# Turning five blocks of constants at another place in the mixer of a four-block decoder

## The chip, the cores and the metric

The kernel runs on one core of one Trainium2 chip. The metric is the time on the device, in microseconds (us), of one execution; the lower, the better.

## What is computed

Two stacks of two layers each run over 256 tokens of width 1024, in float32. Only the first mixer matters here. With `h = rmsnorm(x)` and `p = h @ ev_w_in`, the first 1024 columns of `p` feed a gated block (`u`, `va`), the others a linear recurrence (RWKV-7) over 8 heads of 64:

```python
def rwkv7_time_mix(p, mu, w0, w2, a0, a2, g2, k_k, k_a, r_k, gn_g, gn_b):
    p = p + (shift_prev(p) - p) * mu
    r, k, v, lw, la, lg = split(p)
    w = -softplus(-(w0 + tanh(lw) @ w2)) - 0.5
    decay = exp(-exp(w)); a = sigmoid(a0 + la @ a2); g = sigmoid(lg) @ g2
    kk = heads(k * k_k); kk = kk * rsqrt(max(sum(kk * kk, -1), 1e-24))
    k = k * (1.0 + (a - 1.0) * k_a)
    ...                       # the recurrence over time, then a group norm
    bonus = sum(rh * kh * r_k, -1) * vh
    return (o + bonus) * g
```

The layers behind it use small constant vectors: the weights and biases of a causal convolution (`ff_conv_w`, `ff_conv_b`, `conv_w_2`) and the bias `b_ada_2` of a modulation.

## The kernel before, in words

Each engine has a hand-written queue and works it off in order; semaphores tie them together. The sync engine's queue loads the weights, two megabytes at a time, into two ring buffers. Each chunk is used in halves. ScalarE copies a half in a rounded format (`split_hi`, line 601), VectorE computes the remainder (`split_lo`, line 607), and TensorE multiplies with both parts, three matmuls of 256 columns for one exact product, 48 for a whole half (`pe_tile`, lines 1032 to 1034; `pe_rows`, lines 1047 to 1049). Each call of `w.go()` makes the half that is three ahead of the one about to be used: the halves are, by number, 0 for `lora`, 1 and 2 for `k`, 3 and 4 for `va`, 5 and 6 for `r`, 7 and 8 for `u`, 9 and 10 for `v`, 11 to 14 for the output projection.

The small constants are loaded as rows at the start, in seven blocks (`PRS`, line 647). The kernel needs them down the partitions, so TensorE turns each block (`pe_column`, line 772) into a PSUM bank and VectorE copies it from there into `COL` (`dve_column`, line 778). Blocks 6 and 0 are turned at the very start. Blocks 1 to 5 (three of the convolution's weights, its biases, `b_ada_2`) are first used behind the mixer.

The order of TensorE's queue in the mixer is: `lora`, `k` (2 halves), the small matmuls of the two low-rank gates (`sg`, line 2167), the first half of `va`, the sums of the keys' squares (`nm`, line 2175, which wait for ScalarE's squares of line 1301), the gate `g` (line 2182), the second half of `va`, `r` (2), `ws` (line 2191), `u` with the spatial mix `ya` between (lines 2199, 2204), the first half of `v`, blocks 1 to 5, the bonus sums `rk` (line 2214, two matmuls), the second half of `v`, and the turned `v` (`vt`, line 2222). Then comes the solve of the recurrence, TensorE's small matmuls of lines 2235 to 2396.

PSUM banks are given out ahead of time by `bank_plan`. A ring of six banks (0 to 5) serves the keys in the order in which the plan lists them, and `opened(e, key)` makes TensorE wait until the key that had the bank before has been read out. So the place of a key in the list decides who waits for whom. In the kernel before, in the plan's order:

```
key    rk0  rk1   v1    vt0   vt1
bank   0    1     2     3     4
before v0   col1  col2  col3  col4      (the key that had the bank before)
```

`v0` is read out by VectorE's `mixed(5)` (line 1692), which follows ScalarE's `mixed(5)` (line 1272) in the first half of `v`. The columns are read out by `dve_column`, which stands in VectorE's queue behind the `split_lo` that follows `mixed(5)`, and that one waits for ScalarE's `split_hi` behind its own `mixed(5)`.

GpSimd waits for all seven blocks (`col_turned`) before it writes unit matrices over the place where the rows lay (`tt_eye`, line 1222), then for the bonus sums (`rk_mm`), then for the last half of `v`.

Of the kernel before, what the change touches and what calls it, by code (L numbers as in the profile page):

```python
# [104 lines left out]
TWO = [(n, q) for n in range(2) for q in range(2)]  # L105
# [193 lines left out]
def bank_plan():  # L299
# [12 lines left out]
    norm(0, r, False)  # L312
    P.use(("va", 0), 6)
    P.use(("va", 1), 7)
    for key in [("col", 0), ("lora", 0), ("k", 0), ("k", 1), *(("sg", w, q) for q, w in TWO), ("nm", 0), ("nm", 1),
                ("g", 0), ("g", 1), ("r", 0), ("r", 1), "ws", ("u", 0), ("ya", 0), ("ya", 1), ("u", 1), ("v", 0),
                *(("col", t) for t in range(1, 6)), ("rk", 0), ("rk", 1), ("v", 1), ("vt", 0), ("vt", 1)]:
        P.use(key, r())
    r = Ring(range(8))
    for n in range(2):  # L320
# [121 lines left out]
def program(nc, A, consts, out):  # L442
    with ExitStack() as ctx:
# [61 lines left out]
        def ht(k):  # L505
            return HT1 if k else HT0
# [10 lines left out]

        S = Sems(lambda name: ctx.enter_context(nc.semaphore(name)))
        bank_of = bank_plan()
        bank_sems = [S[f"bank{b}"] for b in range(8)]  # L520

# [4 lines left out]
        def ps_of(key):  # L526
            return PS[bank_of[key][0]]

        def bank_sem(key):
            return bank_sems[bank_of[key][0]]  # L530

        def opened(e, key):
            b, n = bank_of[key]
            if n:
                e.wait_ge(bank_sems[b], n)
            return PS[b]
# [4 lines left out]
        for n, (key, parts) in enumerate(chunks):  # L541
# [5 lines left out]
            if len(parts) == 2:  # L547
                v = r[:, :].rearrange("p (s k n) -> p s k n", s=2, k=NK)
# [20 lines left out]
        def shaped(x, k):  # L569
            if k == NK:  # L570
                return c3(x, NK)
            if k:
                return x.rearrange("p (s k n) -> p s k n", s=2, k=NK)
            return x
# [28 lines left out]
        def split_lo(e, which):  # L603
            for i in which:
                n, v, k, _ = halves[i]
                e.wait_ge(S["w_hi"], i + 1)
                e.tensor_tensor(shaped(WLO[i % NB], k), v, shaped(WHI[i % NB], k).bitcast(F32),  # L607
                                ALU.subtract).then_inc(S["w_lo"], 1)
# [8 lines left out]
        def taken(e, w):  # L617

            i = w.taken
            w.taken += 1  # L620
            e.wait_ge(S["w_lo"], i + 1)
            return WHI[i % NB], WLO[i % NB]
# [10 lines left out]
        col, row_parts, n_rows = {}, [], []  # L633
# [134 lines left out]
        def pe_column(e, t):  # L768
            ps = opened(e, ("col", t))
            e.wait_ge(S[f"rows{t}"], 16 * len(row_parts[t]))  # L770
            k = n_rows[t]
            e.transpose(ps[:, 0:k], PRS[t][0:k, :], CT[0:k, C_ID:C_ID + k]).then_inc(S["col_turned"], 1)
# [3 lines left out]
        def dve_column(e, t):  # L776
            e.wait_ge(S["col_turned"], COL_ORDER.index(t) + 1)
            e.tensor_copy(COL[:, t * 128:t * 128 + n_rows[t]],
                          ps_of(("col", t))[:, 0:n_rows[t]]).then_inc(bank_sem(("col", t)), 1)
# [237 lines left out]
        def flat_k(w, k):  # L1017
            return w[:, 256 * k:256 * k + 256]

        def pe_tile(e, w, key, k_norm, fresh, pair=False, turned=()):  # L1020

            hi, lo = taken(e, w)
            ps = opened(e, key)
            h = ht(k_norm)
            for a in range(2):
                o = ps[:, 256 * a:256 * a + 256]
                for k in range(NK):
                    if fresh and a == 0 and k % 4 == 0:
                        e.wait_ge(S["h_lo"], 4 * k_norm + 3 + k // 4)
                    c = (8 * a + k) * 128 if pair else 256 * k + 128 * a  # L1030
                    wh, wl = hi[:, c:c + 128], lo[:, c:c + 128]
                    e.matmul(o, wh, h[0][:, k, :], start=k == 0, stop=False)  # L1032
                    e.matmul(o, wh, h[1][:, k, :], start=False, stop=False)  # L1033
                    x = e.matmul(o, wl, h[0][:, k, :], start=False, stop=k == NK - 1)  # L1034
                if a == 0 and turned:
                    pe_turn_back(e, k_norm, turned)
            x.then_inc(S["w_used"], 1)

        def pe_rows(e, w, key, k_norm, q):

            hi, lo = taken(e, w)
            h = ht(k_norm)
            for n in range(2):
                ps = opened(e, key(n)) if q == 0 else ps_of(key(n))
                o, t = ps[:, 256 * q:256 * q + 256], slice(128 * n, 128 * n + 128)
                for k in range(NK):
                    e.matmul(o, h[0][:, k, t], flat_k(hi, k), start=k == 0, stop=False)  # L1047
                    e.matmul(o, h[0][:, k, t], flat_k(lo, k), start=False, stop=False)  # L1048
                    x = e.matmul(o, h[1][:, k, t], flat_k(hi, k), start=False, stop=k == NK - 1)  # L1049
            x.then_inc(S["w_used"], 1)  # L1050
# [621 lines left out]
        def vector_program(e):  # L1672
            w = Stream()
# [11 lines left out]
            def mixed(m):  # L1685

                name, o, mu0, q = MIXED[m]
                ps = ps_of((name, q))
                e.wait_ge(S["mix_own"], m + 1)
                for a in range(2):  # L1690
                    t = o[:, 2 * q + a, 1:256]
                    x = e.scalar_tensor_tensor(t, ps[:, 256 * a:256 * a + 255], cc("ev_mu", mu0 + 2 * q + a), t,
                                               ALU.mult, ALU.add)
                x.then_inc(bank_sem((name, q)), 1)
# [23 lines left out]
            e.tensor_tensor(E1, SS[:, :, 0, 64], SS[:, :, 0, 128], ALU.subtract).then_inc(S["e1"], 1)  # L1718
            e.wait_ge(S["e1"], 1)
            e.tensor_tensor(E2, E1, SS[:, :, 1, 64], ALU.subtract).then_inc(S["e2"], 1)  # L1720
            split_lo(e, w.go())
            for q in range(2):
                key = ("nm", q)
# [15 lines left out]
            for n in range(2):  # L1739
                s6, q = st6[:, 6 * n:6 * n + 6], mv[:, 4 * n:4 * n + 4]  # L1740
# [6 lines left out]
            for n in range(2):  # L1747
                q, key = mv[:, 4 * n:4 * n + 4], ("va", n)
# [26 lines left out]
            for q in range(2):  # L1775
                key = ("u", q)
# [14 lines left out]
                                ALU.subtract).then_inc(S["ya_lo"], 1)  # L1791
            mixed(5)
            split_lo(e, w.go())
            for t in range(1, 6):
                dve_column(e, t)
            mixed(6)
            for q in range(2):
                key, v = ("rk", q), Vm[:, 2 * q:2 * q + 2, :]
# [5 lines left out]
            for n in range(2):  # L1804
                for g in range(2):
                    key = ("L", n, g)
# [24 lines left out]
            for i in range(1, 6):  # L1831
                for n in range(2):
                    key = ("Y", i, n)
# [96 lines left out]
            for what, p in OD:  # L1930
                two, t = slice(2 * p, 2 * p + 2), pairs[p % 4]
# [3 lines left out]
                elif what == "s":  # L1935
# [4 lines left out]
                    for g in range(2):  # L1940
                        key = ("od", "s", 2 * p + g)
# [28 lines left out]
            for what, i in MO:  # L1970
# [4 lines left out]
                elif what == "kn":  # L1975
                    k = KR[:, i]
# [6 lines left out]
                    for n in range(2):  # L1983
                        key = ("kr", n) if i else ("first", 4, n)
                        e.tensor_tensor(c3(XN[:, n, 512 * i:512 * i + 512], 4), c3(ps_of(key)[:, :], 4),
                                        bc(k[:, n, :], 128), ALU.mult).then_inc(bank_sem(key), 1)
                elif what == "rq":
                    key = ("rq", i)
# [6 lines left out]
                elif what == "p":  # L1995
                    t = smx[i % 4]
# [6 lines left out]
                elif what == "lo":  # L2003
                    key = ("mo", "o", i)
# [8 lines left out]
            for hh in range(2):  # L2013
                for p in CIN_PART:
                    for q in range(2):
                        key, j = ("cin", p, hh, q), 2 * q
# [6 lines left out]
                        if p == 2:  # L2023
# [3 lines left out]
                            for a in range(2):  # L2027
                                k = m = 4 * hh + j + a
                                u, t = CG[:, j + a, :], CV[:, j + a, :]
# [6 lines left out]
                        elif p == 0:  # L2036
                            k, v = 4 * hh + j, CV[:, j:j + 2, :]
# [112 lines left out]
        def tensor_program(e):  # L2150
            w = Stream()
# [9 lines left out]
            for q in range(2):  # L2161
# [6 lines left out]
                                     LOR[p, 0, :], start=True, stop=True)  # L2168
                x.then_inc(S["lora_mm"], 1)
            pe_rows(e, w, lambda n: ("va", n), 0, 0)  # L2170
            e.wait_ge(S["consts_in"], 16)
            for q in range(2):
                ps = opened(e, ("nm", q))
# [32 lines left out]
                x.then_inc(S["ya_mm"], 1)  # L2206
            pe_tile(e, w, ("u", 1), 0, False)
            pe_tile(e, w, ("v", 0), 0, False)
            for t in range(1, 6):
                pe_column(e, t)  # L2210
            for q in range(2):
                ps = opened(e, ("rk", q))
                e.wait_ge(S["rk_in"], 1)
# [90 lines left out]
            for n in range(2):  # L2304
                key = ("Y64", n)
# [11 lines left out]
            for n in range(2):  # L2317
                key = ("TT64", n)
# [112 lines left out]
            for what, p in OD:  # L2431
# [22 lines left out]
                elif what == "o":  # L2454
# [4 lines left out]
                    for n, c, start, stop in ((0, 0, True, True), (0, 1, True, False), (1, 2, False, True)):  # L2459
                        t = slice(128 * min(c, 1), 128 * min(c, 1) + 128)  # L2460
                        for g in range(2):
                            v = slice(128 * p + 64 * g, 128 * p + 64 * g + 64)
# [111 lines left out]
        @block.vector  # L2574
        def _(e):
            vector_program(e)

        @block.tensor
        def _(e):
            tensor_program(e)  # L2580
# [28 lines left out]
```

## Time and profile before

| | us |
|---|---|
| median of 3 runs (lowest, highest) | 1316.14 (1311.34, 1316.25) |
| the profiled execution | 1313.9 |
| its span, from the first to the last instruction | 1312.1 |
| TensorE busy (share of the span) | 1258.2 (96%) |
| VectorE busy | 944.9 (72%) |
| ScalarE busy | 711.8 (54%) |
| GpSimd busy | 16.8 (1%) |

Busy time is the time in which an engine has at least one instruction in work. Matmuls are pipelined, so their busy times overlap, and what a matmul costs in a row of them is the distance from its start to the next start. PE is TensorE, PEld its weight load, DVE VectorE, ACT ScalarE, POOL GpSimd, SP the sync engine. A float32 matmul that is not split by hand stands in the records as two.

### The profile page before, as it was taken

Reading aid. Unit: us, or ns where it says so; the run is one execution under the profiler, and the core shown is the slowest. Engines: PE = TensorE matmul, PEld = TensorE weight load, DVE = VectorE, ACT = ScalarE, POOL = GpSimd, SP = SyncE. Lnnn points to the kernel's source line nnn. Section 1 sums busy time; section 2 is a strip of 40 time slices with the busy share of each in tenths; the row PEclk is TensorE's granted clock in tenths of the full one; section 3 lists DMA queues with packets and bytes.
Section 4 is the critical chain, followed back from the end, with each engine's and each line's share of the span. In section 5 each row is a group of like instructions: output and inputs, shape, how many; then the busy total and the mean of one; then the engine's idle time right before and its main releaser. Section 6 shows DMA issues by size and latency. Waiting matters only on the chain.

```text
span 1312.1 us, 24165 instructions
## 1 busy us (share of the span) xinstructions
PE 1258.2 (96%) x10251; PEld 1171.3 (89%) x10251; DVE 944.9 (72%) x1268; ACT 711.8 (54%) x1039; POOL 16.8 (1%) x26
## 2 busy tenths in 40 slices
PE   6988999999999999999999998999999999999998
PEld 5877879999989888999998997899998898899997
DVE  5784347988877776988877566699997676677543
ACT  5932447665555566865556555644444654744442
POOL 0002000000000000000000000000000000000000
PEclk9999899999999999999999999999999999999999
DMA  9450227777557526677653535599995365675550
GB/s 315 153 193 2 67 62 260 251 237 237 205 194 258 192 65 206 225 266 239 221 211 104 185 129 181 205 326 340 358 343 210 126 233 188 213 263 182 181 184 32
DMA packets 161572, 263.77 MB, mean 201 GB/s; under 512 B 3565, under 2 KB 95929, under 8 KB 161466
## 3 DMA queue, kind: packets, MB, share of 16 engines
q1 hardware_dynamic: 160586, 259.54, 57.7%
q10 hardware_dynamic: 880, 2.69, 0.7%
q8 instruction: 81, 1.33, 0.4%
q14 instruction: 25, 0.20, 0.0%
HBM read 261.17 MB, written 1.05 MB: 200 GB/s over the span
## 4 chain that ended last, share of the span: by engine, by line
PE 73%; DVE 12%; ACT 5%; DMA 5%; issue 4%; DVEq 0%; SPq 0%; ACTq 0%
PE ps L1061 19%; PE ps L1032 12%; PE ps L1034 12%; PE ps L1033 12%; DVE wlo L607 4%; DVE acc L2079 4%; PE ps L2257 2%; DMA arena<-in_w_ada_dram 2%; ACT whi L601 2%; PE ps L1047 1%; PE ps L1049 1%; PE ps L1048 1%; PE ps L818 1%; PE ps L820 1%; PE ps L819 1%
## 5 line engine op out<-in xcount | busy, mean ns | idle before, releaser
L607 DVE TENSOR_TENSOR wlo<-ring,whi 128x2048 fp32r<-128x2048 f32 x195 | 445.5, 2288 | 114.3 <-ACT whi L601 113.2
L1032 PE MATMUL ps<-ghi,whi 128*128 128x256 f32 x1600 | 449.1, 281 | 0.6 <-DVE wlo L607 0.6
L1034 PE MATMUL ps<-ghi,wlo 128*128 128x256 f32 x1600 | 446.8, 279 | 0.0
L1033 PE MATMUL ps<-glo,whi 128*128 128x256 f32 x1600 | 446.8, 279 | 0.0
L601 ACT ACTIVATE whi<-ring 128x2048 fp32r<-128x2048 f32 x195 | 372.3, 1914 | 96.4 <-PE ps L1061 61.6
L1032 PEld LDWEIGHTS ps<-ghi,whi 128*128 128x128 f32 x1600 | 300.2, 188 | 1.5 <-DVE wlo L607 0.8
L1033 PEld LDWEIGHTS ps<-glo,whi 128*128 128x128 f32 x1600 | 300.0, 188 | 0.7
L1034 PEld LDWEIGHTS ps<-ghi,wlo 128*128 128x128 f32 x1600 | 300.3, 188 | 0.0
L1061 PE MATMUL ps<-whi,yhi 128*128 128x512 f32 x480 | 159.4, 397 | 4.2 <-DVE ylo L1916 1.3
L1061 PE MATMUL ps<-wlo,yhi 128*128 128x512 f32 x480 | 156.3, 391 | 0.0
L1061 PE MATMUL ps<-whi,ylo 128*128 128x512 f32 x480 | 155.9, 390 | 0.0
L2079 DVE SCALAR_TENSOR_TENSOR acc<-arena,small,acc 128x512 f32<-128x512 f32 x168 | 126.2, 751 | 7.1 <-DMA arena<-in_w_ada_dram 1.9
L1061 PEld LDWEIGHTS ps<-whi,yhi 128*128 128x128 f32 x480 | 88.3, 188 | 23.9 <-issue 4.2
L1061 PEld LDWEIGHTS ps<-whi,ylo 128*128 128x128 f32 x480 | 90.2, 188 | 19.3
L1061 PEld LDWEIGHTS ps<-wlo,yhi 128*128 128x128 f32 x480 | 90.4, 188 | 19.0
L2121 DVE SCALAR_TENSOR_TENSOR arena<-arena,cols 128x254 f32<-128x254 f32 (+1 forms) x176 | 74.5, 480 | 20.8 <-ACT arena L1642 19.8
L818 PE MATMUL ps<-whi,ghi 128*128 128x256 f32 x224 | 63.9, 285 | 7.0 <-DVE glo L960 6.9
L2136 DVE TENSOR_TENSOR ylo<-arena,yhi 128x256 fp32r<-128x256 f32 x88 | 37.1, 422 | 44.9 <-ACT yhi L1659 44.7
L1640 ACT ACTIVATE arena<-ps 128x512 f32<-128x512 f32 x44 | 26.3, 598 | 73.5 <-PE ps L1034 71.8
L1646 ACT ACTIVATE arena<-ps 128x256 f32<-128x256 f32 x44 | 16.8, 381 | 84.9 <-PE ps L1034 84.8
L819 PE MATMUL ps<-wlo,ghi 128*128 128x256 f32 x224 | 62.7, 280 | 0.0
L820 PE MATMUL ps<-whi,glo 128*128 128x256 f32 x224 | 62.7, 280 | 0.0
(311 smaller groups left out, 1625.0 us busy)
## 6 DMA issues: line engine op xcount, KB each, us to landing
arena<-in_w_ada_dram SPq DMA_DIRECT2D x48, 1024.0 KB, 6.4
ring<-in_ff_w_up_dram SPq DMA_DIRECT2D x44, 1024.0 KB, 7.6
ring<-in_w_gate_up_dram SPq DMA_DIRECT2D x44, 1024.0 KB, 7.1
ring<-in_ff_w_down_dram SPq DMA_DIRECT2D x10, 2048.0 KB, 7.9
ring<-in_w_down_dram SPq DMA_DIRECT2D x10, 2048.0 KB, 8.1
ring<-in_od_w_qkv_dram SPq DMA_DIRECT2D x6, 2048.0 KB, 7.8
ring<-in_w_qkv_dram SPq DMA_DIRECT2D x6, 2048.0 KB, 7.9
ring<-in_w_in_dram SPq DMA_DIRECT2D x6, 2048.0 KB, 8.0
```

The costliest lines, as they stand in the source:

```text
L601: e.activation(shaped(WHI[i % NB], k), v, ACT.Copy).then_inc(S["w_hi"], 1)
L607: e.tensor_tensor(shaped(WLO[i % NB], k), v, shaped(WHI[i % NB], k).bitcast(F32), ALU.subtract).then_inc(S["w_lo"], 1)
L818: e.matmul(o, h[0][:, c, t], wh, start=c == 0, stop=False)
L819: e.matmul(o, h[0][:, c, t], wl, start=False, stop=False)
L820: x = e.matmul(o, h[1][:, c, t], wh, start=False, stop=c == NK - 1)
L1032: e.matmul(o, wh, h[0][:, k, :], start=k == 0, stop=False)
L1033: e.matmul(o, wh, h[1][:, k, :], start=False, stop=False)
L1034: x = e.matmul(o, wl, h[0][:, k, :], start=False, stop=k == NK - 1)
L1061: x = e.matmul(ps[:, :], YT[l][:, src_k + i, t], w[r][:, i, 512 * h:512 * h + 512], start=first, stop=last)
L2079: e.scalar_tensor_tensor(a, AW[:, k, :], SC[:, k:k + 1], a, ALU.mult, ALU.add).then_inc(S["ada_acc"], 1)
L2121: e.scalar_tensor_tensor(t[a][:, lag:256], z[:, 256 * a:256 * a + 256 - lag], conv_col(f, 2 - lag, a * NF + p), t[a][:, lag:256], ALU.mult ...
L2136: e.tensor_tensor(YT[1][:, p % 8, :], tg[r], YT[0][:, p % 8, :].bitcast(F32), ALU.subtract).then_inc(S["y_lo"], 1)
```

## The change

Blocks 1 to 5 are turned by TensorE, and copied by VectorE, at another place of their queues, and stand at another place of the bank plan: behind the low-rank gates and ahead of the sums of the keys' squares. In TensorE's queue that is behind the first half of `va`, in VectorE's behind the small sums `E1`, `E2` (lines 1718, 1720) and ahead of the `split_lo` of half 6. Nothing else is edited.

```diff
@@ bank_plan
-    for key in [("col", 0), ("lora", 0), ("k", 0), ("k", 1), *(("sg", w, q) for q, w in TWO), ("nm", 0), ("nm", 1),
+    for key in [("col", 0), ("lora", 0), ("k", 0), ("k", 1), *(("sg", w, q) for q, w in TWO), *(("col", t) for t in range(1, 6)), ("nm", 0), ("nm", 1),
                 ("g", 0), ("g", 1), ("r", 0), ("r", 1), "ws", ("u", 0), ("ya", 0), ("ya", 1), ("u", 1), ("v", 0),
-                *(("col", t) for t in range(1, 6)), ("rk", 0), ("rk", 1), ("v", 1), ("vt", 0), ("vt", 1)]:
+                ("rk", 0), ("rk", 1), ("v", 1), ("vt", 0), ("vt", 1)]:
@@ vector_program
             e.tensor_tensor(E2, E1, SS[:, :, 1, 64], ALU.subtract).then_inc(S["e2"], 1)
+            for t in range(1, 6):
+                dve_column(e, t)
             split_lo(e, w.go())
@@ vector_program
             mixed(5)
             split_lo(e, w.go())
-            for t in range(1, 6):
-                dve_column(e, t)
             mixed(6)
@@ tensor_program
             pe_rows(e, w, lambda n: ("va", n), 0, 0)
+            for t in range(1, 6):
+                pe_column(e, t)
             e.wait_ge(S["consts_in"], 16)
@@ tensor_program
             pe_tile(e, w, ("u", 1), 0, False)
             pe_tile(e, w, ("v", 0), 0, False)
-            for t in range(1, 6):
-                pe_column(e, t)
             for q in range(2):
                 ps = opened(e, ("rk", q))
```

The bank plan that follows from it, in the plan's order, from the moved blocks on:

```
key    col1 col2 col3  col4  col5  nm0   nm1  g0   g1   r0   r1   ws   u0   ya0  ya1
bank   1    2    3     4     5     0     1    2    3    4    5    0    1    2    3
before k0   k1   sg0,0 sg1,0 sg0,1 sg1,1 col1 col2 col3 col4 col5 nm0  nm1  g0   g1

key    u1   v0   rk0   rk1   v1    vt0   vt1
bank   4    5    0     1     2     3     4
before r0   r1   ws    u0    ya0   ya1   u1
```

From `rk0` on every key has the bank that it had in the kernel before.

## Rows read from the trace of the kernel before

**Rows 1.** The page's first part: busy time, share of the span, instructions.

```profile
PE 1258.2 (96%) x10251; PEld 1171.3 (89%) x10251; DVE 944.9 (72%) x1268; ACT 711.8 (54%) x1039; POOL 16.8 (1%) x26
```

**Rows 2.** Chain that ended last, 86 to 110 us: start, us, what.

```profile
88.38 0.47 ACT mix L1272
88.85 1.81 ACT whi L601
90.68 2.29 DVE wlo L607
92.97 0.17 DVE cols L778
```

**Rows 3.** Timeline, 87 to 102 us: start, us, engine, line, out<-in, idle before.

```profile
87.69 0.28 PE L1034 MATMUL ps<-hhi,wlo 128*128 128x256 f32 x1
...
87.81 0.57 PE L772 MATMUL ps<-consts_sb,pre 88*128 88x88 f32 x5
...
88.97 0.87 DVE L1692 SCALAR_TENSOR_TENSOR mix<-ps,cols,mix 128x255 f32<-128x255 f32 x2
...
89.89 1.12 PE L2214 MATMUL ps<-pre,consts_sb 128*128 128x512 f32 x2 [1.50 <-DVE mix L1692]
...
93.19 1.82 PE L2214 MATMUL ps<-pre,consts_sb 128*128 128x512 f32 x2 [2.17 <-DVE cols L778]
...
101.28 0.28 PE L1034 MATMUL ps<-hhi,wlo 128*128 128x256 f32 x1
```

**Rows 4.** Windows: length, busy of PE, PEld, DVE, ACT, POOL, granted clock, DMA.

```profile
44.20:45.65 1.45, 0.00 (x1) 0.03 (x1) 1.45 (x5) 1.44 (x4) 0.00 (x0) 1.00 1.02 390
...
88.40:93.20 4.80, 1.14 (x3) 0.31 (x3) 3.95 (x7) 2.25 (x3) 1.63 (x2) 1.00 0.89 290
93.50:96.90 3.40, 3.40 (x12) 2.44 (x11) 0.29 (x2) 0.00 (x0) 1.18 (x2) 0.50 0.56 176
...
103.70:107.10 3.40, 3.24 (x16) 2.95 (x15) 0.05 (x1) 0.72 (x2) 1.55 (x2) 0.50 0.00 0
```

**Rows 5.** Timeline, 41 to 49 us, around the keys' squares.

```profile
41.67 1.62 ACT L1294 ACTIVATE mix<-ps,cols 128x256 f32<-128x256 f32 x4
...
43.88 0.28 PE L1049 MATMUL ps<-whi,hlo 128*128 128x256 f32 x1
44.60 1.71 ACT L1301 ACTIVATE pre<-mix,cols 128x256 f32<-128x256 f32 x4
...
45.65 1.96 PE L2175 MATMUL ps<-pre,consts_sb 128*128 128x512 f32 x4 [1.49 <-ACT pre L1301]
...
46.21 0.17 DVE L1720 TENSOR_TENSOR small<-small,pre 128x4 f32<-128x4 f32 x1
...
47.44 1.89 PE L2182 MATMUL ps<-pre 128*128 128x256 f32 x8
...
48.13 2.29 DVE L607 TENSOR_TENSOR wlo<-ring,whi 128x2048 fp32r<-128x2048 f32 x1 [1.76 <-ACT whi L601]
```

**Rows 6.** Timeline of the sync engine's queue: issue of the last block's rows.

```profile
10.48 0.35 SPq L647 DMA_DIRECT2D pre<-in_b_ada_dram  x1
```

**Rows 7.** The area that holds the rows, by tile: its transfers, from issue to landing.

```profile
DMA to landing us min/median/max: 7.0/7.8/8.4
```

**Rows 8.** Timeline of VectorE, 92 to 94 us: the five copies.

```profile
92.89 0.90 DVE L778 COPY cols<-ps 128x88 f32<-128x88 f32 x5
```

**Rows 9.** Timeline of VectorE, 77 to 82 us.

```profile
77.38 1.67 DVE L1772 SCALAR_TENSOR_TENSOR pre<-mix,cols 128x256 f32<-128x256 f32 x4
...
81.35 0.68 DVE L1780 TENSOR_TENSOR xn<-xn,ps 128x512 f32<-128x512 f32 x1
```

**Rows 10.** Timeline of TensorE, first and last of the 48 matmuls of half 7.

```profile
66.48 0.36 PE L1032 MATMUL ps<-hhi,whi 128*128 128x256 f32 x1
...
72.11 0.28 PE L1034 MATMUL ps<-hhi,wlo 128*128 128x256 f32 x1
```

**Rows 11.** Timeline of TensorE, 103 us: the turned v.

```profile
103.44 3.50 PE L2222 MATMUL ps<-consts_sb,mix 128*128 128x128 f32 x16 [1.88 <-issue]
```

## The prediction

> **What bounds the kernel now.** I read the page's first part first: TensorE is busy for 96% of the span, VectorE for 72%, ScalarE for 54% [rows 1]. So only idle time or slow time of TensorE can give anything back, and the question is whether the five moved blocks cause such time. Next I asked for the chain of waits around the place they are taken from. Between the end of the first half of v and the second sum of the bonus it leaves TensorE: ScalarE's own share of v (0.47 us), ScalarE's rounding of half 13 (1.81), VectorE's remainder of half 13 (2.29), and the first column copy (0.17) [rows 2]. None of this is data that the bonus sums need. The timeline shows how it gets onto the path [rows 3]. The last matmul of half 9 starts at 87.69, the five transposes follow at 87.81, then TensorE waits twice: 1.50 us for bank 0, which v0 holds until mixed(5) is done, and 2.17 us for bank 1, which column block 1 holds. The last matmul of half 10 starts at 101.28.
>
> The windows add a third loss [rows 4]. In the 4.8 us from 88.4 to 93.2 TensorE worked for 1.14 us, and from 93.5 to 96.9, when it was busy throughout, its granted clock was 0.50, the 1.2 GHz level; in the gap at 44.2 to 45.65 it stayed at 1.00, the 2.4 GHz level.
>
> **What is added at the new place.** TensorE's last matmul of va's first half starts at 43.88; the keys' sums start at 45.65, after 1.49 us of idle time that ScalarE's squares end [rows 5]. Five transposes took 0.57 us [rows 3], in front of which their banks must be free and their rows there. Rows: the last block is issued at 10.48 [rows 6], the slowest landing of that area took 8.4 us [rows 7], so by 18.9, 25 us early. Banks: blocks 1 and 2 follow k0 and k1, blocks 3 to 5 follow gates; the last gate's read ends at 41.67 + 1.62 = 43.29 [rows 5], and that is a gate whose bank only nm0 takes. So the transposes run from 44.2 to 44.8 and cost nothing; the cover is the wait for the squares, 0.9 us of it is left, and without it they would cost 0.57.
>
> VectorE finishes its small sums at 46.21 + 0.17 = 46.38 and then idles 1.76 us for ScalarE's half 6, until 48.13 [rows 5]. Five column copies took 0.90 us [rows 8]: 46.3 to 47.2, hidden, 0.9 us to spare; without cover, 0.90 on VectorE.
>
> The one new wait on TensorE is nm1's, for bank 1, which block 1 now holds until its copy is done. Four records of the two sums span 45.65 to 47.44, so 0.90 us each, and nm1 began at about 46.55. The copy of block 1 begins at 46.3 to 46.4 and takes a quarter of a microsecond (five overlapping ones make 0.90), so it ends near 46.6 and TensorE follows at 46.65. Cost: 0.1 us. Bounds: 0 if the copy slips in behind line 1720 at once; 0.3 if it starts only at 46.6. Behind nm1 stand g0 (bank 2, block 2, copied by 46.8, wanted at 47.5), g1 (bank 3, block 3, copied by 47.0, wanted at 48.4) and r0, r1 (blocks 4, 5, wanted much later): no cost. Behind these copies on VectorE stands only half 6. SP's queue is passed by nothing and issues nothing more. On GpSimd the unit matrices that wait for all seven columns are written right behind the gates instead of behind 88 us; it is busy for 1% of the span and waits for the bonus sums next, so nothing moves there.
>
> **What is removed at the old place.** After half 9 the bonus sums come at once. Their input (line 1772) is ready at 77.38 + 1.67 = 79.05. rk0 gets bank 0 from ws, read long before; rk1 gets bank 1 from u0, read at 81.35 + 0.68 = 82.03 [rows 9]. Half 10 gets bank 2 from ya0, whose read has to be over before line 1780 can run. Its weights are no condition: the remainder made at 90.68 is three halves ahead, half 13. Step by step:
>
> - rk0 starts where the first transpose stood, 87.81, plus the 0.1 us from nm1: 87.91.
> - The two sums take 47.44 - 45.65 = 1.79 us at the full clock [rows 5]: half 10 starts at 89.70.
> - From the first to the last of 48 matmuls it is 72.11 - 66.48 = 5.63 us at the full clock [rows 10]: the last starts at 95.33.
> - Before, it started at 101.28 [rows 3]. The gain is 5.95 us.
>
> As a cross-check by terms: idle 1.50 + 2.17, the transposes' own part 0.58 (88.39 less 87.81), and half the 3.4 us at half clock, 1.70, make 5.95, and 0.1 goes off for nm1: 5.85. The two agree within 0.1; I take 6.0 as a round number, bounds 5.6 (nm1 at 0.3, a slower start of half 10) and 6.3.
>
> Is it kept? Half 10 is followed by mixed(6) on ScalarE and VectorE. ScalarE is free from 88.85 + 1.81 = 90.66, VectorE from 92.97 once the column copies behind it are gone [rows 2]; they are wanted from 95.6. So VectorE's margin is about 3 us. The solve behind it is one chain from TensorE to the copies and back, fed by no transfer, so it moves forward whole; the later weight loads are released by halves used up, and move with it.
>
> **How this stands to the times.** The span of 1312.1 us has 1.8 us around it, 1313.9 in all: 1313.9 - 6.0 = 1307.9. The median of the runs shown, 1316.14, lies 2.2 above the profiled execution, and less 6.0 it gives 1310.1. I have no reason to favour either and take the middle, 1309.0.
>
> **Rivals.**
>
> *The clock also stays up for the turned v.* The 16 records of line 2222 took 3.50 us [rows 11], at a granted clock of 0.50 [rows 4]. They are 8 matmuls of 128 columns, as many columns as the two sums that took 1.79 us at full clock, so the low level cost 1.7 us here. It came after an idle stretch of 1.88 us; one of 1.49 us at 44.2 brought no fall. In the changed kernel the same 1.88 us follow 7.5 us of work (87.8 to 95.3) without a gap, and if the clock holds, the gain is 7.7 us: 1313.9 - 7.7 = 1306.2. Against it: the idle stretch itself is not shorter, and the last 4.6 us before it were fully busy before too. The Trainium skill ("TensorE: Matmul & The Clock Gate", The HAM clock gate) says that the activity monitor runs freely and doesn't start with the kernel, so that one kernel pays a different number of slow matmuls from run to run. By that rule this 1.7 us comes and goes in both kernels, and only a part of it would show between medians; the trace of one execution can't show it.
>
> *Half 10 must wait for its weights.* If the remainder made at 90.68 were half 10's own and not three ahead, it would start at 92.97, not 89.70: 3.3 us less, a gain of 2.7, 1311.2 from the profiled time. For it speaks only that this remainder stands right in front in the chain [rows 2]; against it, the count of halves.
>
> *The gain is given back later in the mixer.* VectorE or GpSimd, not TensorE, would have to end the next wait. VectorE's margin of 3 us speaks against it. It would leave anything from 0 to 3 us; at 0 the time is 1313.9 to 1316.1.
>
> *Slower: a column's rows are late.* TensorE's queue is in order, so a row block that has not landed by 45.65 holds the keys' sums and all behind them, one for one. It eats the whole gain from 45.65 + 6.0 = 51.65 on and makes the kernel slower by over 0.5% from about 58 on, 39 us later than the landing worked out above. I see nothing that could do it.
>
> **Chances and range.** The forecast (gain 5 to 7) gets 0.55, the clock as well (7 to 8.5) 0.25, weights 0.05, given back 0.12, slower 0.03. The low end is the clock case from the profiled time, 1306.2, less 1.2 because medians of this kernel have runs 5 us apart: 1305.0. The high end is the weight case from the median, 1316.14 - 2.7 = 1313.4. What a measurement can tell from no change is about 0.5%, 6.6 us. That lies inside the forecast's own range: against the median of 1316.14 the predicted 1309.0 is 7.1 us less (0.54%), while the gain as summed is 6.0 (0.46%). So I give the forecast half to each side: faster 0.25 + 0.27 = 0.52, same 0.28 + 0.05 + 0.12 = 0.45, slower 0.03.
>
> **What would show it.** Right: five transposes between 44.2 and 44.8 with the keys' sums still at 45.65; column copies at 46.3; no idle time of TensorE between half 9 and half 10 and a clock of 1.00 there; rk1's wait gone from the chain; the last matmul of half 10 near 95.3. Wrong: an idle row in front of nm1 of more than 0.3 us; half 10 released by VectorE's remainder at 93.0; mixed(6) starting late behind 95.6 although its matmul is done; or later stages that start less than 6 us earlier, with an idle row that was not there before. A line 2222 of 1.8 us would be the clock's case.

## The result, and the profile after

The changed kernel took 1305.11 us (median of 8 executions, 1302.08 to 1308.58) against 1312.49 for the kernel before (8 executions, the three shown earlier among them, 1310.0 to 1316.6). The ratio is 0.9934, with a 95% interval of 0.9918 to 0.9951: 0.66% faster, which is 8.7 us of 1312; the medians lie 7.4 us apart. It went the way that was forecast and by the steps that were named, but by more than the 6.0 us that were summed, and from a lower level: 1309.0 plus 6.0 puts the kernel before at 1315.0, and 86 executions of it, taken together, average 1313.5. One execution in all that follows, 1342.79 us with the fillers at the bonus sums, lies 2.5% above the others of its kernel and counts in no ratio or mean, only in that kernel's median.

The page's first line of the changed kernel has TensorE 4.4 us less busy at the same count of instructions [rows 1]:

```profile
PE 1253.8 (96%) x10251; PEld 1167.9 (90%) x10251; DVE 944.3 (72%) x1268; ACT 711.6 (55%) x1039; POOL 15.9 (1%) x26
```

Timeline of the changed kernel around the keys' squares, for [rows 5] (L2177 is the keys' sums, L2184 the gate g):

```profile
43.48 0.28 PE L1049 MATMUL ps<-whi,hlo 128*128 128x256 f32 x1
...
43.59 0.58 PE L772 MATMUL ps<-consts_sb,pre 88*128 88x88 f32 x5
...
45.44 2.07 PE L2177 MATMUL ps<-pre,consts_sb 128*128 128x512 f32 x4 [1.26 <-ACT pre L1301]
...
46.08 0.90 DVE L778 COPY cols<-ps 128x88 f32<-128x88 f32 x5
...
47.34 1.89 PE L2184 MATMUL ps<-pre 128*128 128x256 f32 x8
...
47.92 2.29 DVE L607 TENSOR_TENSOR wlo<-ring,whi 128x2048 fp32r<-128x2048 f32 x1 [0.94 <-ACT whi L601]
```

The transposes stand in the wait, which is still ended by ScalarE's squares. They began 0.6 us sooner than the 44.2 of the prediction: 0.4 because TensorE was that much earlier in this execution (43.48 against 43.88), and the rest because they follow the last matmul by 0.11 us and don't wait for its end. From the keys' sums to the gate g it is 1.90 us instead of 1.79: that is the new wait for the copy of block 1, 0.11 us. VectorE's copies end 0.94 us before its next work can begin.

Timeline where the blocks were taken away, for [rows 2, 3, 11]:

```profile
81.22 0.28 PE L1032 MATMUL ps<-hhi,whi 128*128 128x256 f32 x1
...
86.55 0.28 PE L1034 MATMUL ps<-hhi,wlo 128*128 128x256 f32 x1
...
86.67 1.88 PE L2214 MATMUL ps<-pre,consts_sb 128*128 128x512 f32 x4
...
87.98 0.68 PE L1032 MATMUL ps<-hhi,whi 128*128 128x256 f32 x1
...
93.71 0.28 PE L1034 MATMUL ps<-hhi,wlo 128*128 128x256 f32 x1
...
94.89 0.87 DVE L1692 SCALAR_TENSOR_TENSOR mix<-ps,cols,mix 128x255 f32<-128x255 f32 x2 [2.97 <-ACT mix L1272]
95.87 3.55 PE L2222 MATMUL ps<-consts_sb,mix 128*128 128x128 f32 x16 [1.88 <-issue]
```

TensorE goes from half 9 (last start 86.55) to the bonus sums and half 10 without an idle row. From the last matmul of half 9 to that of half 10 it is 7.16 us; before it was 101.28 - 87.69 = 13.59 [rows 3]. VectorE's margin in front of mixed(6) is 2.97 us, as worked out. The 1.88 us in front of the turned v are as before.

Windows of the changed kernel (the number behind POOL's count is the granted clock), for [rows 4]:

```profile
86.70:93.70 7.00, 7.00 (x53) 6.04 (x52) 4.71 (x6) 2.64 (x3) 1.17 (x2) 1.00 0.81 268
...
96.10:99.50 3.40, 3.32 (x16) 3.02 (x15) 0.00 (x0) 0.64 (x2) 1.57 (x2) 0.50 0.00 0
```

The clock is full where it was 0.50 before; at the turned v it fell in this execution too, so the rival of the clock did not happen here. The two profiled spans differ by 8.7 us (1312.1 and 1303.4). Laid over each other, matmul by matmul, the changed one is 0.4 us ahead at the end of half 3, in front of all that was moved, 1.1 at the end of half 9, 7.6 at the end of half 10, and 8.7 at the end; the last 1.1 us come in small steps from 520 us on (7.8 ahead at 526, 8.0 at 1012, 8.6 at 1135). The 0.4 and these steps belong to the two executions compared; nothing here shows that the change makes them.

### The profile page after: what moved, and what is told of

Same layout as the page of the kernel before. It is cut to its first block, busy times and chain, and to the rows that moved or that the text cites. A ratio compares the mean times of both kernels' runs of the same rounds, so it can differ in the third digit from the quotient of the medians.

```text
span 1303.4 us, 24165 instructions
## 1 busy us (share of the span) xinstructions
PE 1253.8 (96%) x10251; PEld 1167.9 (90%) x10251; DVE 944.3 (72%) x1268; ACT 711.6 (55%) x1039; POOL 15.9 (1%) x26
## 4 chain that ended last, share of the span: by engine, by line
PE 74%; DVE 12%; DMA 5%; ACT 5%; issue 4%; DVEq 0%; SPq 0%; ACTq 0%
PE ps L1061 19%; PE ps L1032 12%; PE ps L1034 12%; PE ps L1033 12%; DVE acc L2079 4%; DVE wlo L607 4%; DMA arena<-in_w_ada_dram 3%; PE ps L2257 2%; ACT whi L601 2%; PE ps L1047 1%; PE ps L818 1%; PE ps L820 1%; PE ps L1048 1%; PE ps L819 1%; PE ps L1049 1%
## 5 line engine op out<-in xcount | busy, mean ns | idle before, releaser
L1640 ACT ACTIVATE arena<-ps 128x512 f32<-128x512 f32 x44 | 26.3, 598 | 73.5 <-PE ps L1034 71.9
```

## The experiments

Each median stands with its ratio and interval; other times are means over the executions compared. For each kernel the mean granted clock is given too, because it differs between executions, and the time with it. From the clock c of an execution follows how long it ran at half rate: 2 x (1 - c) x span, called low clock below. "Without low clock" is where a straight line through the executions, time against low clock, meets zero. The experiments ran in four comparisons, and the kernel before averaged 1313.3, 1314.4, 1313.4 and 1313.4 us in them, so a difference of 1 us between means of different comparisons says little.

**The two kernels again.** No edit. Expected of the kernel before:

> The kernel before, unchanged, to see what differs between two executions of one kernel. Theory A (the change gains 6.0 us by bank waits, transposes and low clock, and the rest of the measured 8.7 us is luck of the profiled executions): ratio 1.000 within 0.2%; the profile may show the matmuls of halves 5, 8, 9 and 10 at 0.113 us apart as the changed kernel had them, instead of 0.118, and low clock at other places. Theory B (the change itself made these matmuls closer): they stay at 0.118 apart here.

Expected of the changed kernel:

> The changed kernel again. Theory A: ratio to before 0.9945 (7 us less), the last matmul of half 10 near 94 us, and the distances of matmuls vary from one execution to the next. Theory B: distances of 0.113 us in halves 5, 6, 8, 9 and 10 again.

Before again: 1312.04 median, ratio 0.9990 (0.9977 to 1.0003). Changed again: 1306.40 median, ratio 0.9941 (0.9922 to 0.9960). Neither theory held for the matmuls' distances: the kernel before had 0.113 us in half 5, against B, and 0.118 in halves 8, 9 and 10, against A; the changed kernel had 0.113 in all that B names. All executions of each whose clock is on record, together:

```
                executions   mean time   mean clock   low clock   time at no low clock (straight line)
before          86           1313.5      0.9938       16.3 us     1308.0, plus 0.34 us per us of low clock
changed         15           1305.4      0.9969        8.0 us     1302.8, plus 0.32 us per us of low clock
```

The gain is 8.2 us on average, 5.2 of it without the clock and 3.0 with it (0.34 x 16.3 less 0.32 x 8.0). With executions drawn anew from these, 95% of the draws lie between 6.9 and 9.4 for the gain, 4.0 and 6.4 for the part without the clock, and 1.4 and 4.4 for the clock's. The four executions of before at a clock of 0.999 average 1308.7, the five of the changed kernel at 0.999 or 1.000 average 1302.9.

The profiled execution of the kernel before again had a low stretch of 6.8 us where the first had 3.4, and another at the turned v:

```profile
90.80:97.60 6.80, 5.89 (x21) 4.86 (x22) 1.51 (x6) 0.00 (x0) 1.17 (x2) 0.50 0.52 165
...
104.50:111.30 6.80, 5.26 (x148) 5.00 (x148) 2.33 (x5) 1.62 (x4) 0.42 (x1) 0.50 0.01 2
```

What the longer one costs stands in its timeline, from the second bonus sum to the last matmul of half 10:

```profile
91.71 2.08 PE L2214 MATMUL ps<-pre,consts_sb 128*128 128x512 f32 x2 [1.54 <-DVE cols L778]
...
100.94 0.28 PE L1034 MATMUL ps<-hhi,wlo 128*128 128x256 f32 x1
```

That is 9.23 us; in the first profile it was 101.28 - 93.19 = 8.09 [rows 3].

**The old place, another bank.** The five blocks go through bank 6, behind `va`, and leave the ring.

```diff
-                *(("col", t) for t in range(1, 6)), ("rk", 0), ("rk", 1), ("v", 1), ("vt", 0), ("vt", 1)]:
+                ("rk", 0), ("rk", 1), ("v", 1), ("vt", 0), ("vt", 1)]:
         P.use(key, r())
+    P.use("five", 6)
...
-            for t in range(1, 6):
-                pe_column(e, t)
+            pe_five(e)        # all five into bank 6; VectorE copies them in the old place
```

> The five blocks are turned and copied at the old place, but into one bank outside the ring (bank 6, free since the gated block's norm), so that the two bonus sums and half 10 get banks read long before. Theory A (bank waits): both idle rows of 1.5 and 2.2 us and the low clock behind them go, only the five transposes' 0.58 us stay: 5.4 us less than before, last matmul of half 10 at 95.9, 0.6 us behind the changed kernel. Rival (the place in front of the keys' sums matters by itself, for example because the wait there is filled): 3 us or more slower than the changed kernel.

Measured: 1305.62 median, ratio 0.9945 (0.9926 to 0.9964), 7.2 us less than before where 5.4 were expected; low clock 8.7 us, 1303.1 us without it. From half 9 to the bonus sums there is no idle row:

```profile
88.36 0.58 PE L789 MATMUL ps<-consts_sb,pre 88*128 88x88 f32 x5
88.78 1.91 PE L2229 MATMUL ps<-pre,consts_sb 128*128 128x512 f32 x4
```

So the banks' release is what the change is worth, not the place in front of the keys' sums: at the old place with a free bank the kernel is as fast as the changed one within the intervals. The place itself can bring the transposes' 0.6 us, which these intervals can't resolve.

**TensorE kept busy in the old waits.** Needless matmuls, whose results nobody reads; all waits stay.

```diff
+        def fill(e, cols):
+            e.wait_ge(*read_out(("va", 0)))
+            for c in cols:
+                e.matmul(PS[6][:, 0:c], CT[:, C_BLK:C_BLK + 128], CT[:, C_BOD:C_BOD + c], start=True, stop=True)
...
             for q in range(2):
+                fill(e, ((512, 256), (512, 512))[q])
                 ps = opened(e, ("rk", q))
```

> The kernel before with four needless matmuls (results never read, bank 6): 512 and 256 columns in the wait in front of the first bonus sum, twice 512 in front of the second. The waits stay, TensorE is only kept busy. Theory A with the clock as its own term of 1.7 us: the low clock from 93.5 to 96.9 goes, half 10 ends 1.7 us earlier, ratio 0.9987. Rival (the clock costs nothing beyond the waits, or it falls at another place instead): same time as before within 0.5 us, or slower by the fillers.

Measured: 1309.35 median, ratio 0.9970 (0.9958 to 0.9982). Low clock 5.2 us instead of 16.3, and 1307.7 us without it, as the kernel before (1308.0) within the scatter. The waits still end with the same two engines:

```profile
89.82 1.12 PE L2220 MATMUL ps<-pre,consts_sb 128*128 128x512 f32 x2 [0.18 <-DVE mix L1697]
...
93.12 1.12 PE L2220 MATMUL ps<-pre,consts_sb 128*128 128x512 f32 x2 [0.46 <-DVE cols L778]
...
99.62 0.28 PE L1039 MATMUL ps<-hhi,wlo 128*128 128x256 f32 x1
```

and the clock behind them is full:

```profile
93.70:99.60 5.90, 5.90 (x49) 5.66 (x48) 0.03 (x1) 0.00 (x0) 1.18 (x2) 1.00 0.29 89
```

The fillers save 4 us, more than twice the 1.7 that theory A gave them. It missed by size, not by kind. Not all of the 4 us are paid at this place, for in the profiled execution the low stretch at the turned v was gone too. What is paid here the traces tell. From the second bonus sum to the last matmul of half 10 it is 6.50 us at full clock (99.62 less 93.12), and 8.07, 8.09, 8.93, 9.16 and 9.23 in the five profiled executions of kernels with the same waits and no fillers in them. So a low stretch of 3.4 us (two executions) costs 1.6 us here and one of 6.8 us (three) 2.4 to 2.7, 2.2 on average.

**The first bonus sum behind half 9's result.** The changed kernel with one bank exchanged.

```diff
-        P.use(key, r())
+        bank = r()
+        P.use(key, 5 if key == ("rk", 0) else bank)
```

> The changed kernel, but the first bonus sum gets bank 5, behind half 9's own result (v0), as it stood behind v0 in the kernel before. Theory A (bank waits set the gain, the clock adds to each wait): TensorE idles from 86.7 until mixed(5) has read v0 at about 89.0, 2.3 us, and up to 1.7 us of low clock come behind it: 2.3 to 4.0 us more than the changed kernel, ratio to before 0.996 to 0.997. Rival (only the wait for the columns mattered): as the changed kernel, 0.994.

Measured: 1307.23 median, mean 1308.1, ratio 0.9957 (0.9941 to 0.9973), a little under the 0.996 to 0.997 expected; 2.7 us more than the changed kernel's mean; without low clock 1305.2 against 1302.8. The one wait of 2.24 us came back, released by mixed(5):

```profile
89.25 0.70 PE L2215 MATMUL ps<-pre,consts_sb 128*128 128x512 f32 x1 [2.24 <-DVE mix L1693]
```

**The copies ahead of half 13's remainder.** The kernel before, VectorE's order alone changed.

```diff
             mixed(5)
-            split_lo(e, w.go())
             for t in range(1, 6):
                 dve_column(e, t)
+            split_lo(e, w.go())
             mixed(6)
```

> The kernel before, but VectorE copies the five columns right behind mixed(5), ahead of the remainder of half 13. TensorE's first wait (1.5 us) and the transposes stay, the second wait (2.2 us) should go. Theory A: 2.2 us for the wait and part of the clock's term, 0 to 3 us, because 1.5 us of idle time is left: 2.2 to 5 us less than before, ratio 0.996 to 0.998. Rival (only the place ahead of the keys' sums helps): 1.000.

Measured: 1308.35 median, ratio 0.9957 (0.9942 to 0.9973), by which it is 5.6 us faster, a little over the range given. The second wait is gone and both sums run together; low clock 9.4 us instead of 16.3, and 1305.3 us without it, 2.7 less than before, where the wait was 2.2. The wait for `mixed(5)` was 2.14 us in this execution, not 1.50; the kernel before had 2.13 in one of its three profiles, so that is not this edit's.

```profile
89.86 3.07 PE L2214 MATMUL ps<-pre,consts_sb 128*128 128x512 f32 x4 [2.14 <-DVE mix L1692]
```

**A filler ahead of the turned v**, in the changed kernel:

```diff
             pe_tile(e, w, ("v", 1), 0, False)
+            fill(e, (512, 384))
             e.wait_ge(*read_out(("v", 0)))
```

> The changed kernel with two needless matmuls of 512 and 384 columns (results never read, bank 6) in the 1.88 us of idle time ahead of the turned v. Theory A with a larger clock term (low clock behind a wait costs 0.3 to 0.5 of its length, and the changed kernel has 7 us of it per execution on average): the low stretch at the turned v never occurs, mean granted clock up from 0.997 to 0.998 or more, 1 us less than the changed kernel. Rival (the low stretch only moves to the solve's waits, or costs nothing): no difference.

Measured: 1303.16 median, ratio 0.9921 (0.9900 to 0.9941), mean 1303.4 against 1305.4; low clock 3.9 us instead of 8.0. The intervals of this ratio and of the changed kernel's (0.9922 to 0.9960) overlap, so the 2 us are likely and not certain. The profiled execution had no low stretch in the mixer or the solve at all.

**The same filler in the kernel before:**

> The kernel before with the filler of 512 and 384 columns ahead of the turned v alone. Theory A (low clock behind each wait by itself): the stretch at the turned v goes, that at the bonus sums stays; mean granted clock 0.994 to 0.996 and 1 to 2 us less than before, ratio 0.9985 to 0.9992. Rival (the stretch at the turned v in the kernel before comes from the waits at the bonus sums): no difference, 1.000.

Measured: 1310.05 median, ratio 0.9976 (0.9967 to 0.9985), 3.4 us less than before, more than the 1 to 2 expected; low clock 7.3 instead of 16.3 us. The rival fell: the stretch at the turned v can be taken away with the bonus sums' waits in place. But the two are not separate either, as theory A had it. The fillers at the bonus sums take away 11 us of low clock and this one 9, together more than the 16.3 there are, so taking one stretch away often takes a part of the other with it.

**Fillers in two more waits of the solve:**

```diff
                 ps = opened(e, key)                     # key is ("TT64", n)
+                if n == 0:
+                    e.matmul(ps[:, 0:512], CT[:, C_BLK:C_BLK + 128], CT[:, C_BOD:C_BOD + 512], start=True, stop=True)
...
             def sa(n):
+                if n == 0:                              # 512 and 128 columns into a bank of the output sums
...
```

> As the one with a filler ahead of the turned v, and needless matmuls in two more waits behind the solve as well (512 columns ahead of the last corner blocks, 512 and 128 ahead of the first solved product). Theory A: granted clock 0.999 or 1.000 in nearly every execution, and a time near the 1302 us that the changed kernel has in its own executions at clock 1.000: 2.5 us less than the changed kernel's mean, ratio to before 0.991 to 0.992. Rival (fillers cost as much as the clock gives): 0.994.

Measured: 1303.79 median, ratio 0.9924 (0.9902 to 0.9945). No gain over the single filler: low clock fell to 3.0 us, but its two executions at clock 1.000 took 1303.9 and 1302.8 us, those with one filler 1301.5 to 1302.7. These two fillers give nothing that can be measured; theory A expected 0.991 to 0.992. Its profiled execution had its only low stretch in the mixer and solve at 75.8 us, far ahead of all three fillers.

**One filler, and ScalarE's copies ahead of its rounding:**

```diff
-            split_hi(e, w.go())
             for n in range(2):
                 key = ("Y64", n)
                 e.wait_ge(S["y64_mm"], n + 1)
                 e.activation(L12[n][64:128], heads_of(key)[64:128], ACT.Copy).then_inc(bank_sem(key), 1)
+            split_hi(e, w.go())
```

> The changed kernel with the filler ahead of the turned v, and one step of ScalarE's queue moved: its rounding of half 14 comes behind the copies of the corner blocks (Y64) instead of ahead of them, because TensorE waits 1.11 us there for a copy that stands behind 1.9 us of rounding. Theory: the 1.11 us go, 1303.4 - 1.1 = 1302.3 on average, ratio to before 0.991. Rival (the wait moves to the next copies, which wait for the same queue): 0.992 as without the move.

Measured: 1301.62 median, ratio 0.9917 (0.9899 to 0.9934): the fastest of all, 1302.4 on average against 1303.4 with the filler alone (the intervals overlap). In the changed kernel the copies followed the rounding, and TensorE idled for them:

```profile
142.72 1.91 ACT L601 ACTIVATE whi<-ring 128x2048 fp32r<-128x2048 f32 x1
...
144.66 1.08 ACT L1396 ACTIVATE pre<-ps 64x512 f32<-64x512 f32 x2
145.35 2.04 PE L2325 MATMUL ps<-solve,pre 64*64 64x64 f32 x32 [1.11 <-issue]
```

Here the copies come first, and the idle part is gone:

```profile
141.02 1.17 ACT L1400 ACTIVATE pre<-ps 64x512 f32<-64x512 f32 x2
...
142.22 1.91 ACT L601 ACTIVATE whi<-ring 128x2048 fp32r<-128x2048 f32 x1
142.59 2.07 PE L2331 MATMUL ps<-solve,pre 64*64 64x64 f32 x32
```

**Each kernel once more, for the places of low clock and the matmuls' distances:**

> The kernel before once more, for where the clock is low: theory A expects a low stretch of 3.4 or 6.8 us beginning between 90 and 94 us, and distances of 0.118 us in halves 8 and 9.

> The changed kernel once more: no low stretch between 80 and 95 us, distances of 0.113 us in halves 8, 9 and 10.

Before: 1313.76, low stretches from 93.45, 103.7 and 154.9. Changed: 1307.73, low stretches from 96.4 (6.8 us) and 147.6 (10.2 us), none between 80 and 95. The distances were as expected. The low stretch at the bonus sums stands in all three profiles of the kernel before and in none of the changed one's three. Half 9 of the kernel before, first and last start, against 81.22 and 86.55 above:

```profile
81.92 0.28 PE L1032 MATMUL ps<-hhi,whi 128*128 128x256 f32 x1
...
87.46 0.28 PE L1034 MATMUL ps<-hhi,wlo 128*128 128x256 f32 x1
```

5.54 us against 5.33, for the same 48 matmuls at the same full clock. Halves 8 and 9 were at 0.118 us apart in every profiled execution of a kernel with the old order (eight), and at 0.113 in seven of eight with the new one; the eighth is the kernel with all fillers. There the clock fell just ahead of half 8, but its matmuls had been 0.118 apart in every half before that too. Half 5 had 0.118 in five of the eight with the old order and in that one with the new.

**Is it the bank numbers?** The old order with the new banks (the ring skips five), and the new order with the old banks (it skips one):

```diff
+        if key == ("nm", 0):
+            r.i += 5                       # the second kernel: 1
         P.use(key, r())
```

> The kernel before, its order and its waits unchanged, but the keys from the keys' sums to half 9's result stand in the banks that the changed kernel gives them (the ring skips five banks there), and the bonus sums in banks 5 and 0, half 10 in bank 1. Theory D (the bank number decides whether a half's matmuls are 0.118 or 0.113 us apart): 0.113 in halves 8 and 9, 0.4 us less than before. Rival (something in the order of work decides): 0.118 there as in all executions of the kernel before. Time: ratio 0.9995 to 1.000 in either case.

> The changed kernel's order, but the ring skips one bank in front of the keys' sums, so that the keys from there to half 9's result stand in the banks of the kernel before. The first of the keys' sums then waits for the copy of block 1 (about 46.3 to 46.6, TensorE could start at 45.4): 1.1 us more. Theory D: 0.118 us in halves 8 and 9, 0.4 to 0.6 us more; together 1.6 us more than the changed kernel. Rival: 0.113 there, 1.1 us more.

Old order, new banks: 1314.30 median, ratio 1.0002 (0.9990 to 1.0014), distances 0.118. New order, old banks: 1304.29 median, ratio 0.9941 (0.9921 to 0.9960), distances 0.113. The bank numbers did nothing to the distances in either; theory D fell. In the second kernel the first keys' sum waits for the copy of block 1:

```profile
46.50 1.96 PE L2179 MATMUL ps<-pre,consts_sb 128*128 128x512 f32 x4 [1.25 <-DVE cols L780]
```

It starts 1.06 us later than in the changed kernel, and half 10's last matmul came at 94.66 instead of 93.71. Over its four executions the time shows no loss; the trace shows 1 us.

## Why the prediction was off

**Right:** what bounds the place, and each step of the move. The transposes and copies are hidden, nm1's wait is 0.11 us (0.1 predicted), both bank waits and the transposes are gone, VectorE's margin is 3 us, nothing behind the mixer gives the gain back. The experiment at the old place shows the mechanism alone, the one with rk0 behind v0 and the one with the copies first show each wait near its price (2.4 and 2.7 us without low clock, for 2.2 us each).

**The step that failed is the sum of the gain**, 6.0 us where 8.2 were measured (6.9 to 9.4), and first of all its term for the clock. "Half the 3.4 us at half clock, 1.70" took the one low stretch of one execution for the cost. For that execution it was right (8.09 less 6.50 is 1.6), but in three of five the stretch was 6.8 us long and cost 2.4 to 2.7, 2.2 on average at this place. And the sum had no term for the low clock further on, at the turned v and in the solve: over all executions the kernel before runs 16.3 us at half clock and the changed one 8.0, which is worth 3.0 us (1.4 to 4.4) in all. So this term was about 1.3 us too small.

The second part is the clock-free one, 5.95 - 1.70 = 4.25, against 5.2 measured (4.0 to 6.4). The averages can't tell these apart, but the traces can. From the last matmul of half 9 to that of half 10 it is 87.63 to 99.62, 11.99 us, with the old waits at full clock, and 7.16 in the changed kernel: 4.8. The sum had 7.64 here (87.69 to 95.33), 0.5 too long. It laid 1.79 us for the two sums and 5.63 us for a half end to end; in the changed kernel half 10 starts 1.31 us behind the sums' start (87.98 less 86.67), before their records end at 88.55, and takes 5.73. And 0.2 us is the closer distance of the matmuls: the kernel with all fillers, where it was 0.118, took 7.37 us over the same stretch. Halves 8 and 9, first to last matmul, took 10.85 us where they took 11.27, another 0.4 that the sum put at nothing ("rk0 starts where the first transpose stood"). What in the order of work makes the matmuls closer stays open: the bank numbers are excluded, and no other cause was tried. 4.8 and 0.4, less the 0.1 of nm1, make 5.1, near the 5.2 of the averages, and with the clock's 3.0 the 8.2; the agreement is closer than the intervals warrant.

**The level was off too.** "I have no reason to favour either and take the middle" gave the median of three executions, 1316.14, as much weight as the profiled one. It put the forecast 3.5 us under the median of before that was measured beside the changed kernel, where the sum said 6.0. The average of the 86 executions is 1313.5, next to the profiled 1313.9, and less 6.0 that is 1307.5. So of the 3.9 us between the forecast and the measured 1305.11, 1.5 come from the level and 2.2 from the gain. That the measured time still lies within the stated 1305.0 to 1313.4 is owed to the low end, which was set for a rival that did not occur in the profiled execution.

**The clock rival** was put as full clock at the turned v in the changed kernel. The records of the turned v took 3.50, 2.51 and 3.31 us in three executions of the kernel before and 3.55, 2.02 and 3.11 in three of the changed one. So the low clock comes and goes there in both kernels, and where it covers them all it costs 1.5 us, not the 1.7 of the prediction. A filler ahead of them is worth 1.9 us in the changed kernel and 3.4 in the one before, where in the filler's profile the low stretch near 155 us was gone too. The Trainium skill ("TensorE: Matmul & The Clock Gate", The HAM clock gate) has the activity monitor run freely, unrelated to a kernel's start; by that rule the same program pays a different amount from run to run, and the traces agree: the low stretch at the bonus sums began at 93.48, 90.82 and 93.45 in three executions of one kernel and lasted 3.4, 6.8 and 3.4 us. What I missed is that the kernel with fewer idle stretches had fewer of these (8.0 us of low clock against 16.3), so that a part of it does show between means.

The other rivals did not occur: half 10 was not held by its weights (no idle row ahead of it), nothing was given back, and no row block was late.

## What to carry to other kernels

Where a ring of buffers is given out in a list, look for the small user in the list whose read-out stands behind long work on another engine: it holds up whoever gets its buffer next, and moving it, or giving it a buffer of its own, frees that one. Price an idle stretch of TensorE with what the clock costs behind it, and take that from many executions, by time against granted clock, not from one low stretch in one trace. A few needless matmuls in an idle stretch that cannot be removed show the clock's share, and may be worth keeping: here they gave 3 to 4 us in the kernel before, and two further ones in the solve gave nothing.

## What the runs showed of the hardware that was not expected

The same matmuls, 128x256 at full clock, start either 0.1133 or 0.1178 us apart. In the sixteen profiles the distance changed only at a break between stages and held from one half to the next where no break lay between.

The granted clock also fell without an idle stretch. In the kernel with all fillers TensorE was busy for 3.40 of 3.40 us, with bias matmuls of one row and small ones of 128 columns, weight loads filling 1.66 us, and from 75.8 the clock was 0.50:

```profile
72.40:75.80 3.40, 3.40 (x15) 1.66 (x13) 3.40 (x6) 0.60 (x1) 0.00 (x0) 1.00 0.96 388
75.80:79.20 3.40, 3.40 (x16) 3.40 (x17) 3.31 (x5) 1.47 (x2) 0.00 (x0) 0.50 0.22 36
```

The kernel with the five blocks in bank 6 had the same from 75.0. But in the first profile of the changed kernel nothing fell behind a stretch much like it (71.9 to 75.3: busy for 3.40 of 3.40 us, weight loads 1.78), so what sets off the fall stays open.

A microsecond of half clock costs about a third of a microsecond of time here, not a half: over the 86 executions the slope is 0.34. At the bonus sums it is 1.6 us for a stretch of 3.4 and 2.4 to 2.7 for one of 6.8.
